# Two transformer blocks on one core: weight slots in rings of 5 and 6 with the low parts in place, last down projections tile by tile, loops unrolled

## The reference, cut to what matters

```python
def first_block(x, ...):                      # once
    h = rmsnorm(x, ln1_g); proj = h @ w_in    # 1024 x 5120: q, k, v of two attentions, two gates
    oa, ob = dilated_attention(...), banded_attention(..., sinks)
    mix = sigmoid(ga) * (oa @ w_branch_a) + sigmoid(gb) * (ob @ w_branch_b)
    x = x + mix @ w_out
    return x + square(relu(rmsnorm(x, ln2_g) @ w_up)) @ w_down      # hidden width 4096

def second_block(x, ...):                     # two layers
    for l in range(2):
        x = layer_norm(ALPHA * x + 0.5 * swiglu(x, ffn1_in[l], ffn1_out[l]), ln_g[l, 0], ln_b[l, 0])
        mix = hybrid_mixer(x, ...)            # 1024 x 2304 projection, two attentions, 1024 x 1024
        x = layer_norm(ALPHA * x + mix, ln_g[l, 1], ln_b[l, 1])
        x = layer_norm(ALPHA * x + 0.5 * swiglu(x, ffn2_in[l], ffn2_out[l]), ln_g[l, 2], ln_b[l, 2])
    return x
```

## Time and profile before

| what | value |
|---|---|
| median of 3 runs | 1503.52 us |
| all three | 1501.62 to 1503.77 us |
| span of the profiled execution | 1496.8 us |
| its own time beside the span | not on the page; the median is 6.7 us above the span |
| TensorE busy / VectorE / ScalarE / GpSimd | 93% / 57% / 44% / 11% |
| mean granted TensorE clock | 0.970 |
| read from HBM | 238.57 MB, 160 GB/s over the span |

### The profile page before, as it was taken

The page is one execution under the profiler, slowest core; times in us unless marked ns, Lnnn a source line. Parts: engine busy times, 40 slices in busy tenths (PEclk is TensorE's granted clock), DMA queues, the critical chain, the costliest instruction groups (busy, mean ns, idle before and its releaser), DMA issues.

```text
span 1496.8 us, 18384 instructions
## 1 busy us (share of the span) xinstructions
PE 1396.3 (93%) x6550; PEld 1133.8 (76%) x6550; DVE 856.5 (57%) x1126; ACT 658.4 (44%) x905; POOL 159.1 (11%) x190
## 2 busy tenths in 40 slices
PE   6989899999999999899899999799998998899995
PEld 5867777888778888676678888588886766688884
DVE  5574565555564444778564444654556775754546
ACT  4644534444354343357344343344342564344442
POOL 3221001000000000332200000200002411200002
PEclk9999999999999999999899999899998998999998
DMA  7632355555476564360176565275552430475561
GB/s 213 208 128 71 106 162 169 184 204 174 168 239 191 189 191 149 99 216 22 56 243 191 184 194 171 87 253 181 185 181 99 147 135 6 161 255 176 189 196 57
DMA packets 152086, 240.54 MB, mean 161 GB/s; under 512 B 6176, under 2 KB 100400, under 8 KB 152016
## 3 DMA queue, kind: packets, MB, share of 16 engines
q1 hardware_dynamic: 151632, 239.10, 48.8%
q0 software_dynamic: 384, 0.54, 0.4%
HBM read 238.57 MB, written 1.05 MB: 160 GB/s over the span
## 4 chain that ended last, share of the span: by engine, by line
issue 67%; PE 18%; DVE 5%; ACT 4%; POOL 3%; DVEq 2%; DMA 0%; POOLq 0%; SPq 0%; ACTq 0%
PE ps L1256 3%; PE ps L1257 2%; PE ps L1258 2%; PE ps L1248 2%; PE ps L1396 2%; PE ps L1250 2%; PE ps L1249 2%; POOL wlo L388 2%; ACT whi L366 1%; ACT ptb L635 1%; PE ps L1372 1%; DVE wlo L388 1%; PE ps L1364 1%; PE ps L1283 1%; POOL rstd L423 1%
## 5 line engine op out<-in xcount | busy, mean ns | idle before, releaser
L388 DVE TENSOR_TENSOR wlo<-raw,whi 128x2048 fp32r<-128x2048 f32 (+3 forms) x241 | 466.0, 1940 | 451.2 <-ACT whi L366 450.9
L366 ACT ACTIVATE whi<-raw 128x2048 fp32r<-128x2048 f32 (+3 forms) x254 | 409.7, 1620 | 480.6 <-PE ps L1250 392.8
L1248 PE MATMUL ps<-whi,xt_hi 128*128 128x512 f32 (+1 forms) x992 | 391.4, 395 | 5.7 <-DVE wlo L388 5.1
L1250 PE MATMUL ps<-whi,xt_lo 128*128 128x512 f32 (+1 forms) x992 | 383.7, 387 | 0.0
L1249 PE MATMUL ps<-wlo,xt_hi 128*128 128x512 f32 (+1 forms) x992 | 383.2, 386 | 0.0
L1248 PEld LDWEIGHTS ps<-whi,xt_hi 128*128 128x128 f32 x992 | 186.6, 188 | 46.4 <-DVE wlo L388 9.6
L1250 PEld LDWEIGHTS ps<-whi,xt_lo 128*128 128x128 f32 x992 | 186.3, 188 | 38.7
L1249 PEld LDWEIGHTS ps<-wlo,xt_hi 128*128 128x128 f32 x992 | 186.8, 188 | 35.2
L1248 PE MATMUL ps<-whi,ht_hi 128*128 128x512 f32 x432 | 168.0, 389 | 0.0
L1249 PE MATMUL ps<-wlo,ht_hi 128*128 128x512 f32 x432 | 168.0, 389 | 0.0
L1250 PE MATMUL ps<-whi,ht_lo 128*128 128x512 f32 x432 | 168.0, 389 | 0.0
(11 more groups left out here) (161 smaller groups left out, 1295.8 us busy)
## 6 DMA issues: line engine op xcount, KB each, us to landing
raw<-in_ffn_w_in_dram SPq DMA_DIRECT2D x180, 512.0 KB
raw<-in_ffn_w_out_dram SPq DMA_DIRECT2D x44, 1024.0 KB
raw<-in_w_in_dram SPq DMA_DIRECT2D x36, 768.0 KB
raw<-in_w_up_dram SPq DMA_DIRECT2D x16, 768.0 KB
raw<-in_w_in_dram SPq DMA_DIRECT2D x18, 512.0 KB
raw<-in_w_out_dram SPq DMA_DIRECT2D x12, 768.0 KB
raw<-in_w_down_dram SPq DMA_DIRECT2D x8, 1024.0 KB
raw<-in_w_down_dram SPq DMA_DIRECT2D x16, 512.0 KB
```

The lines of the kernel that those rows point to most:

```text
L366: act.activation(whi[slot][:, 0:n, 0:width], raw[slot][:, 0:n, 0:width], ACT.Copy).then_inc(hi_done[slot], 1)
L388: dve.tensor_tensor(wlo[slot][:, 0:n, 0:width], raw[slot][:, 0:n, 0:width], whi[slot][:, 0:n, 0:width].bitcast(F32), ALU.subtract).then_in ...
L1248: pe.matmul(o, hi[:, k, tok], whi[slot][:, b, 0:width], start=start, stop=False)
L1250: m = pe.matmul(o, lo[:, k, tok], whi[slot][:, b, 0:width], start=False, stop=stop)
```

## The change

- **Slots.** There are seven slots of `raw` and `whi`, and `wlo` lies on `raw`: the low part overwrites the raw data. Buffers are placed by hand so that the ring shares space with others that are dead at the time. Every weight unit has 4 blocks of 512 columns (or 8 of 256), numbered `u` in the order of use; `SLOT_OF[u]` is a ring of 5 slots up to the MLP of block 1 and of 6 from there on. A load waits until the matmuls of the unit before it in its slot are through; `split_hi` waits for the transfer alone. One counter each (`hi_done`, `lo_done`, `used`) replaces those of the slots.
- **Strips** are 4+4 blocks. In block 1's attention seven full units are split at fixed steps (`STEP_SPLITS`), those of both branch projections among them.
- **First strips.** A first tile multiplies the high part of x with high and low parts of all 8 blocks, and then the low part of x, with the transposes of tile 1 placed before its last four matmuls and behind them. Transposes go to banks 4 to 7.
- **Stage ends.** At the end of a gated feed-forward the down projection of the last but one chunk is held back and runs tile by tile with the last one; the first transposes of the next stage stand before the last three matmuls. At the end of the MLP the last chunk's down projection runs by tile and half, and its hidden part is transposed between the two units before it.
- **POOL** splits nothing any more. The splits of the next stage's first two units are ACT's and DVE's, before the norm. The variance constant is added on DVE.
- **Loops.** All hardware loops are unrolled; copies of the layer's small constants go away.

```diff
+FIRST_RING, RING = (0, 1, 2, 3, 4), (2, 3, 5, 6, 0, 1)
+SLOT_OF = [FIRST_RING[u % 5] if u < U_MLP else RING[(u - U_MLP) % 6] for u in range(U_ALL)]
+STEP_SPLITS = {2: 16, 5: 17, 8: 18, 10: 19, 12: 20, 14: 21, 16: 22}
...
+        raw = [sb(f"raw{j}", [P, UB], at=a) for j, a in enumerate(raw_at)]
+        wlo = [sb(f"wlo{j}", [P, UB], F32R, at=a) for j, a in enumerate(raw_at)]
+        whi = [sb(f"whi{j}", [P, UB], F32R, at=a) for j, a in enumerate(hi_at)]
...
+        def load(sp, u, dst, src):
+            if EARLIER[u] is not None:
+                sp.wait_ge(used, EARLIER[u] + 1)
+            sp.dma_start(dst, src).then_inc(loaded[SLOT_OF[u]], 32)
...
+        def split_hi(act, u):
+            j = SLOT_OF[u]
+            act.wait_ge(loaded[j], 32 * TURN[u])
+            act.activation(whi[j][:, :], raw[j][:, :], ACT.Copy).then_inc(hi_done, 1)
...
         def norm_pool(pool, q):
             for t in range(TT):
                 pool.wait_ge(var_ready, 2 * q + t + 1)
-                pool.tensor_tensor(lrs[:, t:t + 1], mv[:, t, 1:2], ln_eps[:, :], ALU.add)
-                pool.drain()
                 pool.tensor_tensor(lrs[:, t:t + 1], lrs[:, t:t + 1], half[:, 0:1], ALU.pow).then_inc(lrs_ready, 1)
-                if t == 0 and mix is not None:
-                    ...
-                if t == 0:
-                    split_lo(pool, 1, T, n)
-                if t == 0 and last:
-                    split_lo(pool, 2, T, STRIP[2])
...
+        def ffn_dve(dve, u, g, after):
...
+            chunk(FFN_S - 2)
+            e = FFN_S - 1
+            split_lo(dve, u + ffn_down(e))
+            for v in after[:1]:
+                split_lo(dve, v)
+            hidden_dve(dve, g + e, e % 2, True, (0,))
+            for v in after[1:]:
+                split_lo(dve, v)
+            ht_dve(dve, g + e, e % 2, True, (0,))
+            hidden_dve(dve, g + e, e % 2, True, (1,))
+            ht_dve(dve, g + e, e % 2, True, (1,))
...
# norm_dve, order of work: add, statistics of tile 0; centre(0); scale(0)
+            if ffn:
+                add(1, 0)
+                stat(1, 0)
+            add(1, 1)
+            stat(1, 1)
+            variance(1)
+            if not last:
+                xt_dve(dve, n, toks=(0,))
             centre(1)
             scale(1)
...
# block 2, after the attention
-                split_lo(dve, 0, t + L_WOUT + 1, 3)
-                split_lo(dve, 1, t + L_WOUT + 1, 3)
...
+                for v in (u + L_WOUT + 2, u + L_WOUT + 3, u + L_FFN2, u + L_FFN2 + 1):
+                    split_lo(dve, v)
...
+        def first_tile(pe, n, u, t, bank, before_last=None):
+            o, tok = ps[:, bank, :], slice(t * P, (t + 1) * P)
+            for k in range(KD):
+                if k % 4 == 0:
+                    pe.wait_ge(xt_hi_done, 4 * n + 2 * t + k // 4 + 1)
+                    if t == 0:
+                        pe.wait_ge(lo_done, u + k // 4 + 1)
+                pe.matmul(o, xt_hi[:, k, tok], block_of(whi, u + k // 4, k % 4), start=k == 0, stop=False)
+                pe.matmul(o, xt_hi[:, k, tok], block_of(wlo, u + k // 4, k % 4), start=False, stop=False)
+            for k in range(KD):
+                if k % 4 == 0:
+                    pe.wait_ge(xt_lo_done, 4 * n + 2 * t + k // 4 + 1)
+                if k == 4 and before_last is not None:
+                    before_last()
+                m = pe.matmul(o, xt_lo[:, k, tok], block_of(whi, u + k // 4, k % 4), start=False, stop=k == KD - 1)
+                if t == TT - 1 and k % 4 == 3:
+                    m.then_inc(used, 1)
...
# ffn_pe, the last down projections (before, end: units of the last two chunks)
+            for t in range(TT):
+                for k in range(2):
+                    for h in range(2):
+                        m = down_tile(pe, before, k, h, t, False, False, k, 1 - par)
+                if t == 0:
+                    hid_tile_pe(pe, g + e, par, 1, True)
+                    pe.wait_ge(lo_done, end + 1)
+                else:
+                    m.then_inc(used, 1)
+                pe.wait_ge(ht_lo_done, 2 * (g + e) + t + 1)
+                for h in range(2):
+                    for k in range(2):
+                        if t == h == k == 1 and late is not None:
+                            late()
+                        m = down_tile(pe, end, k, h, t, False, k == 1, k, par)
+                    m.then_inc(used if t == h == 1 else y_done, 1)
...
-            with pe.Fori(0, LAYERS) as l:
+            for l in range(LAYERS):
```

More of the change, by code:

```diff
@@ L182, in build @@
+        rope1 = square2
+        mixed = proj1[:, :, DM:2 * DM]
+        mix_b = proj1[:, :, 2 * DM:3 * DM]
+        ps = ctx.enter_context(nc.psum_tensor("ps", [P, 8, BW], F32))
+        loaded = [sem(f"loaded{j}") for j in range(len(raw))]
+        hi_done = sem("hi_done")
+        lo_done = sem("lo_done")
+        used = sem("used")
         x_loaded = [sem(f"x_loaded{t}") for t in range(TT)]
@@ L734, in _ @@
             read_gate(act, S1_GATES)
[L735 to L736 removed]
+            read_qk(act, True, 0, range(6), 4, QK1_TILES, 4)
+            reads = gate_reads()
             for i in range(UNITS + 2):
@@ L1018, in scale @@
                                              ALU.mult, ALU.add).then_inc(xt_src, 1)
-            halves = range(2) if ffn else (1,)
-            for h in range(2):
-                if h in halves:
-                    add(0, h)
-                stat(0, h)
+            if not ffn:
+                for t in range(TT):
+                    add(t, 0)
+                    stat(t, 0)
+            else:
+                add(0, 0)
+                stat(0, 0)
+            add(0, 1)
+            stat(0, 1)
+            variance(0)
+            dve.wait_ge(g_loaded, 32 * (q + 2))
             centre(0)
@@ L1308, in last_strip, with first_strip, tiles_strip @@
+        def first_strip(pe, n, src, u, turned=1):
+            for b in range(turned, 2):
+                xt_half_pe(pe, n, 0, b, src)
+            first_tile(pe, n, u, 0, 0, lambda: xt_half_pe(pe, n, 1, 0, src))
+            xt_half_pe(pe, n, 1, 1, src)
+            first_tile(pe, n, u, 1, 1)
+        def tiles_strip(pe, u, bank0, late):
             for t in range(TT):
                 for k in range(KD):
-                    slot = 0 if k < 3 else 1 if k < 6 else 2
-                    b = k - sum(STRIP[:slot])
@@ L1319, in last_strip @@
+                    if t == 1 and k % 4 == 3:
+                        m.then_inc(used, 1)
                 if t == 0:
-                    m.then_inc(y_part, 1)
-        def xt_pe(pe, n, src, tiles=KD):
-            for t in range(TT):
-                xt_tile_pe(pe, n, t, src, tiles)
-            pe.wait_ge(xt_lo_done, 4 * n + 4)
+                    m.then_inc(y_done, 1)
         def qk_pe(pe, base, events, bank0, banks, src, tiles):
@@ L1407, in hid_tr_pe @@
                 hid_tile_pe(pe, g, par, t, ffn)
-        def ffn_in_chunk(pe, t, par, slot, between=None, part=None):
-            if part is None:
-                pe.wait_ge(lo_done[slot], t + 1)
-            for b in range(4):
-                if part is not None and b == 0:
-                    pe.wait_ge(lo_half, part)
-                if part is not None and b == 2:
-                    pe.wait_ge(lo_done[slot], t + 1)
-                k = 4 * slot + b
-                m = block_mm(pe, xt_hi, xt_lo, k, slot, b, pair(par), k == 0, k == KD - 1)
-                if b == 3:
-                    m.then_inc(used[slot], 1)
-                if b == 1 and between is not None:
-                    between()
@@ new lines, in down_tile, with down @@
+        def down_tile(pe, u, k, h, t, first, last, kh, par):
+            return tile_mm(pe, ht_hi[par], ht_lo[par], kh, u, 2 * k + h, t, 4 + 2 * t + h, first, last)
+        def down(pe, units, g, par, first=False, between=None):
+            pe.wait_ge(ht_lo_done, 2 * g + 2)
+            for i, u in enumerate(units):
+                if i == 1 and between is not None:
+                    between()
+                pe.wait_ge(lo_done, u + 1)
+                for k in range(2):
+                    for h in range(2):
+                        for t in range(TT):
+                            m = down_tile(pe, u, k, h, t, first and i == k == 0, False, 2 * i + k, par)
+                m.then_inc(used, 1)
@@ new lines, in _ @@
+            for t in range(TT):
+                pe.wait_ge(ht_lo_done, 2 * e + t + 1)
+                for h in range(2):
+                    for k in range(4):
+                        if t == h == 1 and k == 3:
+                            xt_half_pe(pe, XT1, 0, 0, xres)
+                        m = down_tile(pe, mlp_down(e) + k // 2, k % 2, h, t, False, k == 3, k, e % 2)
+                        if t == h == 1 and k % 2 == 1:
+                            m.then_inc(used, 1)
+                    if t == 0 or h == 0:
+                        m.then_inc(y_done, 1)
```

1149 lines of the change are left out of this document (492 added, 657 removed).

## The result

| | before | after |
|---|---|---|
| median | 1503.64 us (1501.62 to 1506.36, 4 runs) | 1444.94 us (1444.32 to 1446.89, 4 runs) |
| ratio | 1 | 0.9619, 95% interval 0.9602 to 0.9636 |
| span of the profiled execution | 1496.8 us | 1444.9 us |

The forecast was 1454 us from a span of 1447.4, with a range of 1441 to 1475.

What follows compares the result with a forecast made beforehand. TensorE, 93% busy, was taken to lose time only between stages. Gains of 15.5, 12.2, 8.0, 12.0 and 4.0 us, less small costs, made -49.4: span 1447.4, plus 6.7 gives 1454 us, range 1441 to 1475.

Steps and rivals of the forecast that it cites:

- the chain: Stage ends, tile 0: add, statistics, centre, power, scale, transposes, high and low part, first matmul; TensorE waits for it.
- scale pair: The two scale halves in a norm: 4.56 us beside GpSimd's split, put at 1.4 to 1.5 us at tile 0.
- T: Start of tile 0's last down matmul; transposes were put at T+5.0, the first matmul behind them at T+6.6.
- Block 1's attention: 28 blocks split inside it, not 22, on an engine in its chain: +1.5 us, between -2 and +5.
- Feed-forward ends: Stage ends after the first feed-forward: 7.5 us gained in layer 1, 8.0 in layer 2; tile 1 waits 1.7 us.
- The tail: Kernel's end, no next strip: ends T+15.1, 8.0 us gained; sign: 12 to 13 us after tile 0's last matmul.
- Projections and attention of block 2: Block 2's projections and its attention: the same work, so no gain or cost.
- Output projections of block 2: Stage end after the attention's output projection, twice: 6.0 us gained each, of 3 to 7.5; TensorE waits 3.8 us.
- Outside the span: Median of the timed runs lies 6.7 us above the profiled span; this was added to the forecast span.
- Half comes back: First rival: VectorE's longer train at stage ends loses 4 us at seven places, 28 us, giving 1482 us; chance 0.24.
- Straight-line code: Rival: unrolled instructions arriving by DMA starve TensorE; 1534 us at 2 us per fetch; chance of slower 0.06.
- The rings: Weight slots: loads wait for matmuls 5 or 6 units back; 18 us to spare, 12 in ring of five; no cost.

Runs made afterwards that it cites:

- the late split: Against the kernel after: behind the three output projections, the next stage's second unit is split after the first tile's norm, not before; 1435.12 us, ratio 0.9547.

## Why the prediction was right, and where it was not

**What bounds it, and the chain: right.** The same matmuls at the same pace; the gain is all between stages. The scale pair is 1.42 us at all six norms, the transposes and the first matmul stand at the distances from T that the prediction gave them, the clock stays at 1.00 around the gated ends, the issue wait is gone. Putting GpSimd's work back and giving up the held matmuls each brought back the wait that the step names.

**The sum: near in part by luck.** -51.9 us for -49.4 hides two errors that cancel. Block 1's attention came out 9.0 us worse than put, and all other terms together 11.5 us better.

**Feed-forward ends: gains put 1.5 to 2 us too small each.** Tile 1 waited 0.75 us and not 1.7, and the 0.5 us that I set aside for the hidden part behind two splits did not occur. That is nearly all of the -9.1 for -7.5. The tail ended at T+14.2 and not T+15.1; the sign "12 to 13 us" did not fit my own sum and did not come.

**Projections and attention of block 2: put at nothing.** They gained 1.9 and 1.6 us. No run here separates why.

**Output projections of block 2: the term right, its parts not.** I had the next stage's first matmul 5.6 us earlier, and it is: 30.7 us behind the strip's transposes and not 36.4. The gap in it is 2.73 us and not 3.8 (I had named 3 to 4 as a sign), with the clock at 0.74 around it, which I had only allowed for. That VectorE's splits ahead of the norm set it, the late split showed.

**Block 1's attention: the term that failed.** "+1.5, between -2 and +5" was +10.5. I counted VectorE's work (six more blocks) and took its share of the chain from that. The runs show the order: its instruction waits for ScalarE's half of the same unit, and the maxima stand behind it; the same work one step later costs 13 us less. Of the 10.5 us, 4.3 are more time without a matmul (12.1 for 7.8) and 6.2 are slower matmuls, at a clock of 0.91 for 0.98. This was the change's one large loss; everything else together gave 62 us.

**Outside the span: 6.7 us carried over, about 2 found.** I had read the distance of one quick execution from the median as a constant. As a step from a profiled span to a median it did no harm: the median of before less 49.4 is the same 1454. The medians moved 58.7 us, 9.3 more than my sum: 2.5 of it lies in the stages of the two traces, 6.8 in which executions were profiled.

**The clock.** My first rival and two of the expectations charged 1.7 to 2 us of low clock behind each longer wait. In these traces waits of 2.15 to 2.7 us were followed by 0.71 or 0.72 at some places and by 1.00 at others. That is part of why two of the experiments cost less than I expected.

**The rivals.** *Half comes back:* no feed-forward's end shows it. Its mechanism, splits ahead of the norm's chain, is real at the output projections (10.8 us for three) and, with 4 slots, kills the gain. *Straight-line code:* 51 packets of instructions for 40, 138 starts in 30 us as before, and the kernel before without its loops is faster: excluded. The rings cost nothing, as said, but my reason (18 us to spare) spoke only of the dense stretch, where even four slots do.

## What to carry to other kernels

A split in two engines should not have its second half in the same step as its first when something urgent stands behind it: one step's distance was worth 13 us here, the size of the pieces nothing. The depth that a ring needed here was set by the look-ahead that the program order asks for at stage ends, not by the steady state. And a stage end is a chain through several engines on one tile: list its links with their durations, keep GpSimd's SBUF work off VectorE's links, and hold back as many independent matmuls as the chain is long.

## What the runs showed that I had not expected

- One program's span varies by 4.5 us on one chip and 7.4 on another, in step with the granted clock (before: 1497.8 us at 0.972 to 1502.3 at 0.966, and 1497.0 at 0.974 to 1504.4 at 0.965), while what lies outside it stays at 1.8 to 2.9 us.
- A VectorE subtraction in place of its input (2294 ns) is as fast as into a third buffer (2292).
- Who comes first in the race between VectorE and GpSimd can change between two layers of one trace: TensorE waited 5.98 us in layer 1 and 3.26 in layer 2 on the same instructions.
- The granted clock does not follow from a wait's length alone: 2.41 us was followed by 0.72 over 6 us and 2.40 us by 1.00, in one trace.
